# Two-layer mixer kernel, the recurrence of head pairs: right sides among the last level's first products, key mixes and decay sums between the levels

## What is computed

```
def rwkv_streams(rw, dec_w0, dec_up, iclr_a0, iclr_up, k_k, k_a):
    r, k, v = ...                          # slices of the projected input
    wd, ad = tanh(rw[..., WD0:AD0]), rw[..., AD0:GD0]
    kk = heads(k * k_k); kk = kk / norm(kk)
    for d in range(2):                     # forward, backward
        w_log = -softplus(-(dec_w0[d] + wd @ dec_up[d])) - 0.5
        a = sigmoid(iclr_a0[d] + ad @ iclr_up[d])
        kd = k * (1.0 + (a - 1.0) * k_a)
        ...                                # decay exp(-exp(w_log)), kd, a
def step(s, inp):                          # one token of wkv_scan
    sa = einsum('bhij,bhj->bhi', s, -kk_t)
    s = s * w_t + sa * (kk_t * a_t) + v_t * k_t
    return s, einsum('bhij,bhj->bhi', s, r_t)
y = yf + yb; y = group_norm(y) + sum(r * (kf + kb) * r_k) * v; y * (sigmoid(gd) @ g_up)
```

## Time and profile before

| | before |
|---|---|
| median of 3 runs | 3325.36 us (3323.35 to 3326.42) |
| profiled execution | 3319.18 us |
| its span | 3317.4 us |
| PE busy | 3078.1 us, 93% of the span |
| DVE busy | 1578.4 us, 48% |
| POOL busy | 1234.7 us, 37% |
| ACT busy | 564.4 us, 17% |
| chain that ended last, by engine | PE 70%, DVE 14%, DMA 9%, issue 3%, POOL 2%, ACT 1% |

### The profile page before, as it was taken

One profiled execution on the slowest core, in us unless ns is written; L12 is line 12 of the kernel. 1 busy time (PEld: TensorE's weight loads), 2 busy tenths in 40 slices (PEclk: granted clock), 3 DMA queues, 4 the chain that ended last, 5 costly groups with the idle time before them and its releaser, 6 DMA issues.

```text
span 3317.4 us, 69293 instructions
## 1 busy us (share of the span) xinstructions
PE 3078.1 (93%) x32062; PEld 2768.7 (83%) x32062; DVE 1578.4 (48%) x2216; ACT 564.4 (17%) x1042; POOL 1234.7 (37%) x725
## 2 busy tenths in 40 slices
PE   4998998998999999999998788897999999999998
PEld 4877887877887888788698677777989999999998
DVE  4655276446337720378842677776344441113111
ACT  1022202011120120200002445453010000000001
POOL 2000010000000001134274454443648887777774
PEclk7998999998999999999999999999999999999999
DMA  7964288666226634367842000000546554444442
GB/s 269 420 242 181 103 315 317 269 263 241 104 100 241 259 126 183 127 249 297 310 160 91 6 6 9 6 6 26 193 151 233 222 208 169 162 178 147 162 176 101
DMA packets 55921, 583.08 MB, mean 176 GB/s; under 512 B 7202, under 2 KB 9568, under 8 KB 10704
## 3 DMA queue, kind: packets, MB, share of 16 engines
q1 hardware_dynamic: 38080, 466.11, 37.4%
q0 software_dynamic: 17552, 112.54, 8.9%
HBM read 576.52 MB, written 2.10 MB: 174 GB/s over the span
## 4 chain that ended last, share of the span: by engine, by line
PE 70%; DVE 14%; DMA 9%; issue 3%; POOL 2%; ACT 1%; SPq 0%; ACTq 0%; DVEq 0%; POOLq 0%
PE PS L1712 23%; PE PS L374 15%; PE PS L672 7%; PE PS L1665 5%; DMA ring<-in_w_vec_dram 4%; DMA ring<-in_w_second_dram 2%; PE PS L1891 2%; DVE ring L2304 2%; PE PS L417 2%; DMA ring<-in_w_start_dram 1%; PE PS L371 1%; PE PS L1908 1%; PE PS L1906 1%; PE PS L1837 1%; PE PS L1729 1%
## 5 line engine op out<-in xcount | busy, mean ns | idle before, releaser
L374 PE MATMUL PS<-H,ring 128*128 128x256 f32 x2944 | 668.8, 386 | 7.0 <-ACT H L702 7.0
L374 PEld LDWEIGHTS PS<-H,ring 128*128 128x128 f32 x2944 | 562.1, 193 | 94.9 <-issue 17.6
L1712 PE MATMUL PS<-H,ring 128*128 128x128 f32 x3424 | 403.9, 275 | 2.4 <-DMA ring<-in_w_second_dram 2.4
L1712 PEld LDWEIGHTS PS<-H,ring 128*128 128x128 f32 x3424 | 393.9, 192 | 3.2 <-DMA ring<-in_w_second_dram 2.8
L327 POOL DMA_DIRECT2D ring<-in_w_vec_dram x75 | 39.9, 532 | 930.3 <-DVE ring L888 790.5
L2411 DVE TENSOR_TENSOR W<-W,PS 128x256 f32<-128x256 f32 x58 | 24.4, 421 | 676.5 <-ACT W L2049 676.5
L1712 PE MATMUL PS<-H,W 128*128 128x128 f32 x2624 | 317.2, 277 | 10.9 <-POOL W L1541 9.2
L1712 PEld LDWEIGHTS PS<-H,W 128*128 128x128 f32 x2624 | 305.6, 193 | 12.5 <-POOL W L1541 9.9
L1536 POOL TENSOR_TENSOR W<-ring 128x1024 f32<-128x1024 f32 (+1 forms) x74 | 175.2, 2367 | 267.9 <-PE PS L1712 149.3
L672 PE MATMUL PS<-H,ring 128*128 128x256 f32 x1024 | 223.5, 379 | 2.9 <-DVE H L1174 2.9
L672 PEld LDWEIGHTS PS<-H,ring 128*128 128x128 f32 x1024 | 194.2, 190 | 29.9 <-issue 3.7
(11 more groups left out here) (496 smaller groups left out, 5015.5 us busy)
## 6 DMA issues: line engine op xcount, KB each, us to landing
ring<-in_w_second_dram SPq DMA_DIRECT2D x97, 2048.0 KB, 8.1
ring<-in_w_first_dram SPq DMA_DIRECT2D x68, 2048.0 KB, 8.2
ring<-in_w_vec_dram POOLq DMA_DIRECT2D x75, 1024.0 KB, 7.7
ring<-in_w_vec_dram SPq DMA_DIRECT2D x48, 1024.0 KB, 5.0
ring<-in_w_start_dram SPq DMA_DIRECT2D x16, 2048.0 KB, 15.7
H<-in_w_vec_dram POOLq DMA_DIRECT2D x21, 1024.0 KB, 7.9
Pj<-in_w_aside_dram SPq DMA_DIRECT2D x8, 2048.0 KB, 11.3
ring<-in_w_second_dram SPq DMA_DIRECT2D x9, 1536.0 KB, 6.5
```

The source lines that it names most:

```text
L374: mm = pe.matmul(PS[:, t % 2, half * T:(half + 1) * T], ring[:, t % 2, k, half * P:(half + 1) * P], hT[:, k, :], start=(k == 0), stop=(k = ...
L1712: mm = pe.matmul(regions(bank2, r), w[:, k * P:(k + 1) * P], m[:, k, :], start=(first and k == 0 and r // 4 not in opened), stop=(last and ...
```

## The change

Nothing is computed otherwise; instructions move.

- PE: the 32 right-side products move out of `solved` into the first products of level 5. For each cell stand now two right-side products and then two first products.
- ACT: `right_sides` is gone; its two copies stand in `products(j, 5)`, each behind its direction's copy of the first products. `key_mixes` is split by direction: direction 0 goes, with `key_spread`, ahead of `sigmoids(j + 1, 1)`; direction 1 stays behind level 5 and waits as before.
- DVE: `sums(j + 1, 0)` goes from behind level 4 and `normed` to ahead of level 4; `sums(j + 1, 1)` goes from behind level 5 to ahead of it.

```diff
@@ level (PE) @@
                 for u in range(8):
+                    if lev == 5:
+                        for h in halves:
+                            bv = pe.matmul(PS[h, 2 + d, cell(u)], bT[d][h, u, :], VTok[d][h, u % 4, halves[u // 4]], start=True, stop=True)
                     for h, g in zip(halves, other):
                         mm = pe.matmul(PS[h, d, cell(u)], mT[d][g, u, :], xm[d][g, u, :], start=True, stop=True)
+                if lev == 5:
+                    done(bv, "p_bv")
                 done(mm, "p_P")
@@ solved (PE) @@
-            for d in range(2):
-                for u in range(8):
-                    hs = halves[u // 4]
-                    for h in halves:
-                        mm = pe.matmul(PS[h, 2 + d, cell(u)], bT[d][h, u, :], VTok[d][h, u % 4, hs], start=True, stop=True)
-                done(mm, "p_bv")
@@ key_mixes (ACT) @@
-        def key_mixes(j):
+        def key_mixes(j, d):
             need("p_kssq", j, 1)
-            need("p_sig", j, 4)
-            for d in range(2):
-                f("p_tm", TMP[d], AA[d], ACT.Identity, scale=col(j, U_KA), bias=sm[:, j + 80:j + 81])
+            need("p_sig", j, 2 * d + 2)
+            f("p_tm", TMP[d], AA[d], ACT.Identity, scale=col(j, U_KA), bias=sm[:, j + 80:j + 81])
@@ products (ACT) @@
                 f("p_Pc", pm[d], PS[:, d, :].rearrange("p (a b) -> p a b", b=CH), ACT.Copy)
+                if lev == 5:
+                    need("p_bv", j, d + 1)
+                    f("p_bvc", kbv[d][:, :, 64:P], PS[:, 2 + d, :].rearrange("p (u c) -> p u c", c=64), ACT.Copy)
@@ the loop over pairs (ACT) @@
             products(j, 4)
             if after:
+                key_mixes(j + 1, 0)
+                key_spread(j + 1)
                 sigmoids(j + 1, 1)
-                key_spread(j + 1)
             products(j, 5)
             if after:
-                key_mixes(j + 1)
+                key_mixes(j + 1, 1)
                 exponentials(j + 1, 0)
-            right_sides(j)
             solutions(j)
@@ the loop over pairs (DVE) @@
             if before:
                 inverse(j - 1)
+            if after:
+                sums(j + 1, 0)
             level(j, 4)
             if before:
                 normed(j - 1)
             if after:
-                sums(j + 1, 0)
+                sums(j + 1, 1)
             else:
                 ...
             level(j, 5)
             if after:
-                sums(j + 1, 1)
                 keys(j + 1)
                 stream(j + 1)
```

More of the change, by code:

```diff
@@ L2211, in head_roots @@
             f("p_vroot", TL[:, 0, :], TL[:, 0, :], ACT.Sqrt)
[L2213 to L2217, removed]
         def solutions(j):
@@ L2233, in pairs_act @@
         key_spread(0)
-        key_mixes(0)
+        for d in range(2):
+            key_mixes(0, d)
         for d in range(2):
```

## The result

| | before | changed kernel |
|---|---|---|
| median of 7 runs | 3326.42 us | 3339.49 us |
| range | 3316.21 to 3328.74 | 3335.92 to 3354.65 |
| profiled execution | 3319.18 us | 3343.48 us |
| mean granted clock of PE | 0.969 | 0.963 |

The ratio of the two, taken of the mean times, is 1.0047, with a 95% interval of 1.0029 to 1.0065, that is 10 to 22 us. The medians lie 13 us apart and the means 16, where 15.4 us were forecast. All ratios of this document leave out two slow executions, of 4546 and 5273 us. Of these, 4.3 us are there before the first key product (1824.4 against 1820.2), where the change has nothing; they are left out here. From the first key product to the last one it is

A forecast was written before the change was run, and what follows sets the result against it. DVE's string of running sum, key product, stream and steps bounds the pair's second half. Per pair -1.1 +2.1 +1.2 = +2.2 us, seven pairs +15.4, on 3325.4 giving 3341 us; range 3321 to 3347.

The forecast's parts named there:

- its three terms: Per pair with a next one: key product sooner -1.1, collision +2.1, clock +1.2, together +2.2 us.
- Right sides in turn: PE, level 5: right sides and first products in turn fill all four quarters, keeping 2.08 us; 0 more taken.
- Forward sum against the masks: DVE ahead of level 4: sum and subtraction take turns with POOL's masks, level 4's subtractions start 1.8 us later.
- Key product sooner by 1.1 us: DVE behind level 5: key product at 1998.9 instead of 2000.00, a gain of 1.1 us per pair.
- PE's order costs nothing: PE, level 5: right sides add 0 us; the solution waits for DVE's level-5 subtraction, not for PE's order.
- Collision of 2.1 us: DVE's stream: POOL's L1500, 6.1 us behind the key product, takes turns; steps start 9.25 behind instead of 7.15.
- The table of cases in the forecast (6.02, 6.35, 6.54): Starts of DVE's L2533, L2534, L2537 behind the key product, in us; L1500's arrival among them decides what is caught.
- the rival in which the collision is missed: L1500 comes 0.4 us later, at 6.54; DVE keeps its 1.1 us per pair; 3322 us, no change; chance 0.10.
- steps over 9 us behind the key product: Sign in the profile after: DVE's steps start over 9 us behind the key product, where before it was 7.15.
- Clock of 1.2 us: PE stands 4.4 us before the steps' products, then about half clock for 3.4 us; 1.2 per pair, bounds 0 to 1.7.

The follow-up runs named there:

- the run with PE kept busy: Changed kernel plus 10 unread 128x128 products on PE in each of seven pairs, ahead of the steps' forward corrections; mean distance 61.8 us, ratio to before 1.0016.

## Why the prediction was right

The forecast, 3341 us, is 1.5 us off the median. Its mechanism stood: an earlier solution, POOL in DVE's stream, later steps, PE standing, its clock falling behind that. The closeness of the number is luck, since none of its three terms had its size and a fourth was missing.

- *Right sides in turn.* Nearly right. They and the first products took 2.1 to 2.4 us together (in the third pair 2003.57 to 2005.92), where each alone had taken 2.08.
- *Forward sum against the masks.* Right: 2.18+1.58 us with masks of 3.41. No row of before had shown it. The price was 2.0 us, not 1.8: the third pair's first level-4 subtraction, from which the forecast counted, came 2.14 us behind the forward sigmoids' end, where five of the seven pairs had 1.77; now all have 3.76.
- *Key product sooner by 1.1 us.* Right in kind, short in size: counted from the start of the backward sigmoids it comes at 6.19 us in the mean (5.8 to 6.4) instead of 6.92, so 0.7. The step that failed was that PE's order costs nothing. With the right sides in their block and the same sums and mixes it comes at 5.6 us; the right sides alone moved it from 6.9 to 7.5. So the new place of the right sides costs 0.6 us here, and 0.5 with their copies left late. Level 5's second products have a pause of 0.8 to 1.1 us in four pairs and 0.3 to 0.5 in three (rows above), the norms come later and the key product waits for them.
- *Collision of 2.1 us.* Too large in six pairs of seven. L1500 came at 6.48 instead of 6.1 in six pairs, since norms and solution stand directly behind one another on PE: then the solution starts 0.1 us ahead of the key product and not 0.5. It caught one instruction, 1.05 us. In the second pair it came at 6.32 and caught two, 2.1 us, as in the forecast, the small copy among them (below). A mean of 1.2. The table of cases in the forecast (6.02, 6.35, 6.54) was right; the arrival was 0.4 us off, and 0.06 us more would have made the rival in which the collision is missed true. Of the signs named, steps over 9 us behind the key product came in one pair.
- *Clock of 1.2 us.* Right in kind, low in size. PE stood 2.5 to 3.7 us and not 4.4, and yet the fall came in all seven pairs, for up to 6.8 us, and cost 1.9 us by the run with PE kept busy. Another 0.9 us a pair went into the levels (27.2 us from starts to sigmoids, 26.2 before), with more falls behind the starts and more pauses. That was not in the sum.

The copy in the second pair, the only one of the seven above 1 us:

```profile
1951.99 1.25 DVE L2530 COPY H<-W 128x8 f32<-128x8 f32 x1
```

By these terms a pair is -0.7+1.2+1.8+0.9 = +3.2 us, against 3.3 measured and 2.2 forecast. (1.8 is the stretch from steps to starts, 15.36 against 13.52 in the six pairs that the distances span; before, what lay over 13.29 stood beside pauses of PE, without a fall of the clock.) Seven such pairs would be 22 us, where 15.4 were forecast. From the first key product to the last the two profiles differ by 18.8 us, inside the interval of the ratio, 10 to 22 us, and the medians of the whole time by 13.1. The terms are read from one execution of each kernel, so how much of the gap between 13 and 19 us is chance stays open.

## What to carry to other kernels

Before work is brought forward on an engine that has time, follow what it releases to the last engine and ask what runs there at the new moment: here a solution 1.7 us earlier led POOL into the string of DVE instructions that set the pace, and cost 13 us where nothing waited for it. Two engines that take turns by whole instructions make a wait on purpose worth having: one semaphore wait on POOL took the loss away. A stand of PE also has a price behind it, in its clock: 1.9 us a pair here, where the collision itself cost 1.2.

## What was not expected of the hardware

- A tiny copy (8 columns) next to POOL's product took 1.22 us instead of 0.16; its size did not help it. The forward running sum takes turns like a plain two-input instruction. The Trainium skill ("SBUF — State Buffer", Who interferes with whom) says that a VectorE instruction with two SBUF inputs contends with a GpSimd one that reads SBUF. The trace agrees: 2.18 us beside a mask, 1.22 without.
- PE pauses for 0.2 to 2.1 us with no releaser, mostly in dense runs of 64x64 products: between 1840 and 2300 us 32 times before (26.9 us in all) and 41 times (39.3 us) with POOL's wait and eight more products a pair. The key product of the changed kernel moves by 0.6 us from pair to pair with them (5.8 to 6.4 us behind the backward sigmoids), while before it stood at 6.9 in every pair.
